# A two-block transformer on one core: the queries of five heads in front of the expert slots in place of four

## What is computed

```python
q = (xc @ w_query).reshape(PEER_CHUNK, PEER_HEADS, 2, half)      # 8 heads, 2 halves of 128
s = jnp.einsum('thpk,pnk->thpn', q, sub_keys)                    # scores against 2 x 128 keys
sv, si = lax.top_k(s, PEER_TOPK)                                 # 16 best of each half
cand = (sv[:, :, 0, :, None] + sv[:, :, 1, None, :]).reshape(..., 256)
top_s, sel = lax.top_k(cand, PEER_TOPK)                          # 16 best pairs
eidx = jnp.take_along_axis(cidx, sel, axis=-1)                   # expert numbers
g = jax.nn.softmax(top_s, axis=-1)
act = jax.nn.gelu(jnp.einsum('td,thkd->thk', xc, expert_down[eidx]))
out = jnp.einsum('thk,thkd->td', g * act, expert_up[eidx])
```

## Time and profile before

| | |
|---|---|
| runs shown | median 2814.52 us of 3 (2812.45 to 2816.62) |
| the profiled execution | 2814.78 us; its span 2812.9 us |
| busy, share of the span | PE 91%, DVE 51%, POOL 39%, ACT 32% |
| moved over the span | 817.52 MB, mean 291 GB/s; in the slots stages about 420 GB/s |
| gathers | 512 down, 512 up |

### The profile page before, as it was taken

How to read it: one execution, slowest core, us unless ns; L and a number is a source line. 1 busy time by engine, 2 the same in 40 slices (tenths; PEclk the granted TensorE clock), 3 DMA queues, 4 the chain that set the end, 5 groups by cost and what they waited for, 6 DMA issues and landing times.

```text
span 2812.9 us, 29892 instructions
## 1 busy us (share of the span) xinstructions
PE 2557.4 (91%) x9872; PEld 1725.5 (61%) x9872; DVE 1444.7 (51%) x3086; ACT 908.1 (32%) x2255; POOL 1099.2 (39%) x1163
## 2 busy tenths in 40 slices
PE   8898899987988888998998889998887999989999
PEld 6567655433434465676555546574365888857888
DVE  2621776898876436315867767777445100161000
ACT  2241244445553322422444445423333100132000
POOL 0000576676777600003776656766624000070000
PEclk9999999999999999998999999999998999989999
DMA  6475799999999963657999999999931344323444
GB/s 233 171 263 193 318 420 421 420 420 380 410 420 420 420 236 142 253 208 285 420 420 420 420 420 413 421 421 420 421 122 50 132 155 157 136 74 108 156 155 150
DMA packets 187329, 817.52 MB, mean 291 GB/s; under 512 B 20608, under 2 KB 22688, under 8 KB 154160
## 3 DMA queue, kind: packets, MB, share of 16 engines
q0 software_dynamic: 148816, 549.32, 47.9%
q1 hardware_dynamic: 38368, 266.35, 25.4%
HBM read 814.54 MB, written 1.05 MB: 290 GB/s over the span
## 4 chain that ended last, share of the span: by engine, by line
PE 52%; DMA 16%; POOL 13%; DVE 10%; issue 7%; ACT 2%; ACTq 0%; DVEq 0%; SPq 0%; POOLq 0%
PE work L642 43%; PE acc L642 8%; DMA arena<-experts_down,arena 8%; DMA arena<-experts_up,arena 7%; POOL arena L583 7%; POOL arena L610 7%; DVE arena L1753 3%; DVE arena L1668 2%; PE work L716 1%; DVE arena L1591 1%; DVE small L1591 1%; DVE mx L1603 0%; DVE arena L1602 0%; DMA ring<-stream 0%; DMA c<-consts 0%
## 5 line engine op out<-in xcount | busy, mean ns | idle before, releaser
L642 PE MATMUL acc<-arena 128*128 128x512 f32 x1868 | 895.1, 616 | 148.6 <-DMA arena<-experts_up,arena 103.6
L610 POOL DMA_INDIRECT arena<-experts_down,arena x512 | 492.8, 962 | 819.8 <-DVE arena L1737 579.0
L642 PE MATMUL work<-arena,ring 128*128 128x256 f32 x3460 | 767.3, 384 | 25.3 <-ACT arena L1521 14.5
L1753 DVE SCALAR_TENSOR_TENSOR arena<-arena,acc 128x1024 f32<-128x1024 f32 x512 | 618.7, 1220 | 332.6 <-DMA arena<-experts_down,arena 317.1
L642 PEld LDWEIGHTS work<-arena,ring 128*128 128x128 f32 x3460 | 665.6, 193 | 130.6 <-issue 30.8
L642 PEld LDWEIGHTS acc<-arena 128*128 128x128 f32 x1868 | 347.4, 195 | 600.7 <-issue 473.3
L583 POOL DMA_INDIRECT arena<-experts_up,arena x512 | 492.0, 961 | 203.9 <-issue 145.6
L642 PE MATMUL work<-h,ring 128*128 128x256 f32 (+1 forms) x1504 | 335.7, 379 | 12.7 <-DVE h L1591 10.7
L642 PEld LDWEIGHTS work<-h,ring 128*128 128x128 f32 x1504 | 278.1, 195 | 76.4 <-issue 41.2
L1309 ACT ACTIVATE arena<-arena 128x2 f32<-128x2 f32 x256 | 51.9, 203 | 593.4 <-DVE arena L1753 385.6
L642 PE MATMUL work<-lent,ring 128*128 128x256 f32 x992 | 224.5, 379 | 0.0
(11 more groups left out here) (241 smaller groups left out, 1825.2 us busy)
## 6 DMA issues: line engine op xcount, KB each, us to landing
ring<-stream SPq DMA_DIRECT2D x252, 1024.0 KB, 4.9
arena<-experts_down,arena POOLq DMA_INDIRECT x512, 14.5
arena<-experts_up,arena POOLq DMA_INDIRECT x512, 14.6
arena<-na_bias POOLq DMA_DIRECT2D x2, 2048.0 KB, 14.5
arena<-consts POOLq DMA_DIRECT2D x1, 2392.0 KB, 20.3
lent<-consts POOLq DMA_DIRECT2D x2, 1024.0 KB, 15.4
arena<-consts POOLq DMA_DIRECT2D x1, 1816.0 KB, 19.3
x<-x_in SPq DMA_DIRECT2D x1, 1024.0 KB, 5.5
```

The lines of the kernel that those rows point to most:

```text
L610: pool.indirect_dma_start(down[:, (l * PICKS + n) % ROWS, :], None, experts[2 * l], bass.IndirectOffsetOnAxis(ap=expert[:, n:n + 1], axis=0))\
L642: ins = nc.tensor.matmul(o, w, r, start=start, stop=stop, **kw)
L1753: ins = v.scalar_tensor_tensor(row, row, 1.0, tok, ALU.mult, ALU.mult, accum_out=dot[:, n:n + 1])
```

## The change

```diff
@@ -195,7 +195,7 @@
-HEADS_FIRST = 4
+HEADS_FIRST = 5
 LATE_PIECE = 3
```

## The result

| | before | after |
|---|---|---|
| median of 20 runs each | 2812.27 us (2806.88 to 2816.62) | 2815.95 us (2813.90 to 2819.52) |
| ratio | | 1.0016, 95% interval 1.0010 to 1.0023: +4.5 us, 2.8 to 6.5 (the two medians above lie 3.7 us apart) |
| the profiled execution | 2814.78 us, span 2812.9 | 2814.07 us, span 2812.2 |

A forecast was written before the change was run, and what follows sets the result against it. The slots stages were taken as bound by a DMA transfer queue with a fixed number of bytes. Holes of 1.1 us (layer 0) and 3.7 us (layer 1) summed to +4.8 us, so 2819.6 us, range 2811 to 2831.

The forecast's parts named there:

- The chain in front: Start of each slots stage: first exponential, first dot, POOL's ninth down row and PE's first slot 7.80 us later, PE's pause unchanged.
- Between the slots: PE's late matmuls within the slots stage: 7.80 us less work there, PE back at old times by beat 24, no net change.
- The constants' load: Ahead of down row 44 instead of 56 in POOL's queue: wait about 1 us, wait and load costed at 0.
- The queue: DMA requests during POOL's pause at stage start: work lasts until 330.9 us in layer 0, 1327.4 in layer 1.
- The holes: DMA below full rate after POOL's pause: 1.1 us lost near 331 in layer 0, 3.7 near 1329 in layer 1.
- start-up of 2.3 us: Time from POOL's next gather issue until gathers fill the DMA engines again, taken from the very first gather; bounds 0 and twice that.
- the sum by it: Both layers' loss with the skill's 2.0 us fixed transfer time as start-up: 4.2 us.
- the delay passes whole: First rival, slots stages: nothing takes back the 7.80 us in either layer, +15.6, 2830.4 us; chance 0.20.
- no hole opens: Second rival, DMA queue at stage start: it never runs dry, +0, 2814.8 us; chance 0.15.
- The faster rival: Third rival: the constants' load, asked for twelve rows earlier, may hold up nobody; -6.9 us, 2807.9 us; chance 0.12.

## Why the prediction was right

**The chain in front: right to the hundredth.** Forecast +7.80 us for the first exponential, first dot, ninth down row and first slot; the ninth down row is 7.80 us later in both layers, and PE's pause stayed at 7.63.

**Between the slots: right in what it costs, not in the detail.** Beats without late matmuls take 3.5 us (421.05, 7.08 us for two). PE was to be back at its old times by beat 24. At 437.94 it waits 4.82 us for an up row instead, with the constants now ahead of it in the queue. The end of the stage doesn't show it.

**The constants' load: right.** POOL's wait for the last score is 1.77 us in layer 0, forecast 1, from 4.28. Its issue moved from 149.85 to 124.71 us behind the first gather. Rows 44 to 55 land later, dots 44 to 48 by 9.3 us; at slot 56 all but 0.8 is gone. This isn't the late start passed on: with the exponentials first, where POOL starts on time, dots 44 to 48 are still 6.9 us late. It was costed at 0, and that run bears it out, with the load at row 44 and the time of before. The landing of a gather became shorter, 12.6 to 9.2 us in the window of 350 to 400, and 19.1 to 14.2 in that of 425 to 475, where some 11 us had been forecast: right in direction, less in size.

**The queue: right in place, mis-sized in each layer.** The holes are where they were put: POOL issues its ninth down row at the times forecast (327.81 + 1.89 for the shorter front is 329.7). The queue of layer 0 was to end at 330.9, less 1.89 for the front 329.0, that of layer 1 at 1327.4, less 4.10 for the front 1323.3. The engines lost 2.8 and 5.0 us of work against 1.1 and 3.7 forecast. The term that was mis-sized is the start-up of 2.3 us, taken from the very first gather: to give the measured losses it would have to be 3.6 to 4.0 us, within the ends of 0 and 4.6. The GB/s rows of the DMA views of the kernel after, of 320 to 340 and of 1320 to 1340 us, show in steps of 0.5 us where it falls short:

```profile
GB/s 426 418 410 426 401 451 410 418 442 418 451 418 442 434 434 369 426 342 115 166 188 385 361 205 303 344 377 369 295 238 287 360 295 377 344 360 385 385 385 385
...
GB/s 426 442 410 401 451 434 320 123 57 25 16 0 82 106 262 418 270 172 229 369 401 377 336 303 254 344 369 320 360 352 410 401 410 451 401 410 401 401 467 401
```

In layer 0 the rate drops at 329.0, as forecast, and is back at 385 by 330.5; this dip costs 1.0 us, near the 1.1 forecast. In layer 1 it drops at 1323.0, rises 1.3 us behind POOL's issue at 1324.70 and reaches 418 once, at 1327.5; the 5 us from 1323 to 1328 lose 3.3 us, near the 3.7 forecast. So 2.3 us is about right for the dip. The rest of the loss, 1.8 and 1.7 us, comes in the ten us behind it, in which the prediction has the full rate and the windows have 306 and 388 GB/s in layer 1.

A lack of requests doesn't explain those ten us. POOL issues from 1324.70 on with hardly a pause, about one gather per 1.24 us, which is 423 GB/s. By 1338 it has issued eleven, 5.77 MB, while only 4.2 MB moved since 1323, and the engines' busy share is 0.90 and 0.99 in the two windows. So work was waiting while the rate was low. At the very start of a stage, from which the 2.3 us were taken, the 451 GB/s came with the stream's blocks beside the gathers (three in the first 23 us). Whether that makes the difference wasn't tried; why the rate stays low stays open.

A second miss hid the first, by luck. That the change of token tile in layer 0 would give back a part (1 to 2 us, 310 to 326 GB/s before, 340 after) was not foreseen. Stage 0 pays 0.3 to 0.6 us in place of 1.1, within the scatter of its traces, stage 1 4.7 to 4.9 in place of 3.7: sum 5.0 to 5.5 against the 4.8 forecast, and the timed runs 4.5. Without the part given back the sum would be near 7 us. The time forecast, 2819.6, lies 3.7 us above the measured 2815.95. Of that 2.25 us is that before was 2812.27 in the larger set of runs and not 2814.52.

The Trainium skill ("DMA: Bandwidth & Descriptors", Anatomy of one DMA — SWDGE (gpsimd) path) has about 2.0 us of fixed time for such a transfer, and the sum by it was 4.2 us. Its figure is that of one transfer. In layer 1 that sum has 3.4 us, and the dip alone lost 3.3; but with the slow return behind it 5.0 us were lost, so by the runs 2.0 us is too low as the whole price of a restart.

**The rivals.** That the delay passes whole (+15.6) fell with the slots' shifts, +7.8 at slot 8 and +2.2 or +4.9 at slot 100, and with six heads: +7.3 and +9.9 us in the stages in place of +15.6 each. That no hole opens (+0) fell with the windows and with the extra load, whose 2.5 us cost nothing in the hole alone. The faster rival (-6.9) fell with the measured sign; its mechanism fell with the exponentials first, where the load is at row 44 and no hole hides a gain, and the dots of slots 84 to 124 are 0.15 us early in layer 0 and on time in layer 1. Exponentials ahead of the last query also show, on the chip where before takes 2812 us, that the cause is POOL's late ninth gather and not PE's late start.

## What to carry to other kernels

Where a stage is bound by a full transfer queue, moving work between engines costs or gives nothing until the queue runs dry: work out the bytes asked for, less those moved, and set the time they last against the issuer's longest pause, with some 4 us for coming back (3.6 to 4.0 would have fitted here). If it does run dry, put the first weights or exponentials that free the issuer ahead of the work added, not behind it, and then look for the issuer's next wait: here it was 3.6 us and covered on one chip, 8.2 us and not covered on another. And count the bytes in such a stage: each MB moved out of it to where the DMA engines have room was worth some 2.4 us here (10.9 us in the two stages for 4.55 MB), and no other edit tried was faster than before.

## What the runs showed of the hardware

A queue that has run dry does not come back at once: 141, 306 and 388 GB/s in three windows of 5 us before 417. The busy share is 0.90 and 0.99 in the second and third, so the share alone looks nearly full when the rate is not, and POOL had by then asked for more than had moved. Why the rate stays low at that share wasn't tried.

One chip ran every version of the kernel 2 to 3% slower than the others (2874 us for before), with 138 us of POOL's waits ended by nothing that its trace shows; there the same change cost 12 us, and the edit that undid it elsewhere gave nothing in the timed runs, with a second pause of POOL of 8.23 us that emptied the queue in layer 1. A price of a few us measured on one chip need not hold on the next.
